# Two differential attentions in a transformer kernel: probabilities combined two steps ahead, head norms one step later, Silu in pairs, and y rows handed to the output projection as they come

## The chip, the cores and the metric

The kernel runs on one core of a Trainium2 chip. The time is device time in microseconds (us), a median over runs of the same program. The engines have their own instruction streams and wait for one another by semaphores: TensorE (PE in the profile, its weight loads PEld), VectorE (DVE), ScalarE (ACT), GpSimd (POOL), and SyncE (SP), which issues most DMAs.

## The reference

Two transformer blocks in float32 over 256 tokens of width 2048. The first block has two layers. Each layer normalises its input, multiplies by `w_in`, and mixes three branches, each with a Silu gate: attention, pooling and convolution. Layer 0 does it for 256 tokens of x and 256 of a context; layer 1 for x alone (the keys and values still cover both). What the change touches:

```python
def _diff_attention(q, k, v, lam):          # 8 heads, per head two scores of depth 64
    s = jnp.einsum('bqhcd,bkhcd->bhcqk', qq, k).astype(jnp.float32) * scale
    p = jax.nn.softmax(s, axis=-1)
    a = p[:, :, 0] - lam * p[:, :, 1]
    return jnp.einsum('bhqk,bkhe->bqhe', a.astype(v.dtype), v)
...
    y_att = (_rmsnorm(o, subln_g) * (1.0 - lam_init)).reshape(B, L, ATT_WIDTH)
    ...
    y = jnp.concatenate([y_att * jax.nn.silu(g_att),
                         y_pool * jax.nn.silu(g_pool),
                         y_conv * jax.nn.silu(g_conv)], axis=-1)
    return y @ w_out
```

## The kernel before

All large products go by units of weights: one unit is 128 output features by 2048 inputs (1 MB). SyncE loads a unit into `RAW`, ScalarE rounds it in two halves into `WH` (`high`), GpSimd subtracts to get `WL` (line 538), and TensorE makes three matmuls for each of 16 blocks: high by high, high weight by low activation, low weight by high activation (lines 574 to 576). Buffers are two deep, and the semaphores `high_ready`, `split_ready` and `halves_done` tie the three engines together. A unit has 48 matmuls: 512 columns wide in layer 0, 256 wide in layer 1.

Each layer's attention (the functions `attention(l)`, one in each engine's stream) is a hand-written software pipeline over steps `g`. Layer 0 has J = 4 query tiles per head, so 32 steps; layer 1 has J = 2, so 16 steps. `h = g // J` is the head and `s = g % J` the tile in it; in this text the steps of a head are its first, second, third and fourth. A step of TensorE is: transpose the combined probabilities of step g (line 793), scores of step g+2 (line 761), at some steps one of rotate (lines 734, 735, for the rotary embedding of a later head), `out_back` (line 769, transposes a finished head's output back) and `turn_v` (line 742, transposes the next head's values), then `gate_part`, a piece of the sixteen gate units (half a unit in layer 0, a whole one in layer 1), and last the product with the values (line 825). ScalarE copies the transposed probabilities, takes the exponentials of step g+2, does the norm of the last head's output (`head`: squares, Ln, Exp), the Silu of the gate tiles and the `high` of the weights. VectorE finds the maxima of the scores (1754), combines the two softmaxes (`RECIPROCAL` 1789, 1791, 1792, semaphore `at0_comb` or `at1_comb`), applies the rotary embedding, finishes the head norm (1763 to 1766 and a multiply, semaphore `_on`) and multiplies by the gates (1775, and `gate_mul`).

In what order VectorE does this is the point of contact. Step g of VectorE begins with the combination of step g itself; then come the maxima of g+2 and the other work. In the first step of each head that other work ends with `head(h-1)`, which waits for ScalarE's `_rr`:

```python
                if s == 0 and h:
                    head(h - 1)
                if s == 1 and h:
                    gated(h - 1)
```

After the last step, ScalarE and VectorE split the mixed rows y into `HH` and `HL` in four pieces of four tiles, and TensorE starts the output projection (`residual_tiles`), 16 tiles of `w_out`. Between these tiles it makes the modulation vectors of later stages (`mod_unit`, line 552, 1 MB of weights each), one before each tile in layer 0 (from a single buffer, `BUF_OUT0`), two before each in layer 1 (four buffers). SyncE issues the first of these loads after `at{l}_y` has reached 8, that is after the last head is gated, and each further one when TensorE has read a buffer. ScalarE issues the reload of x (`xin`, two pieces of 2 MB) at the end of layer 0's attention.

## Time and profile before

| | us |
|---|---|
| median of 3 runs | 3447.99 (3447.86 to 3456.14) |
| the profiled execution, its own time | 3441.95 |
| its span | 3440.2 |
| TensorE busy | 3184.4 (93%) |
| GpSimd busy | 1890.8 (55%) |
| ScalarE busy | 1488.4 (43%) |
| VectorE busy | 1263.8 (37%) |

Busy time is the sum of an engine's instructions; a stretch in which TensorE is busy at half its clock counts as busy too. The first attention (layer 0) lies at about 576 to 885 us of the span, the second (layer 1) at about 1508 to 1722 us, and each is followed by its output projection.

### The profile page before, as it was taken

To read this page: it belongs to the slowest core of one execution; us is meant where nothing else is said; L and a number is where in the kernel's file an instruction comes from. 1 tells how busy PE (TensorE), PEld (TensorE's weight loads), DVE (VectorE), ACT (ScalarE), POOL (GpSimd) and SP (SyncE) were. 2 spreads that over 40 slices of the span, in tenths; PEclk is the share of its full clock that TensorE was granted. 3 is DMA by queue.
4 is the path that set the end of the run, shared out by engine and by line. 5 is a ranking of instruction groups with operands and counts; after the bars stand their busy time and mean duration, and the time that the engine had idled before them with its cause. 6 is when DMAs were issued, how large, how long until landed. Compare 5 with 4: busy or idle time off the path is not lost.

```text
span 3440.2 us, 64483 instructions
## 1 busy us (share of the span) xinstructions
PE 3184.4 (93%) x25962; PEld 2845.4 (83%) x25962; DVE 1263.8 (37%) x2045; ACT 1488.4 (43%) x2186; POOL 1890.8 (55%) x756
## 2 busy tenths in 40 slices
PE   6899999998799996997799899999989999999999
PEld 4788886776677895876688788889989999999999
DVE  2148303444201418035412876667251443333000
ACT  3222223556322431256634566556534555554333
POOL 1244543222233557443344555566776888887887
PEclk9999999999899998998899999999999999999999
DMA  9786222111443781222196576544444455554555
GB/s 393 305 331 262 98 98 75 60 62 50 171 153 141 308 327 54 94 109 75 60 357 254 189 249 239 199 147 147 171 159 159 171 183 183 182 184 171 183 195 183
DMA packets 85970, 613.35 MB, mean 178 GB/s; under 512 B 9536, under 2 KB 10816, under 8 KB 12736
## 3 DMA queue, kind: packets, MB, share of 16 engines
q1 hardware_dynamic: 84672, 606.02, 47.7%
q10 hardware_dynamic: 1152, 5.24, 0.4%
q8 instruction: 109, 1.79, 0.2%
q14 instruction: 37, 0.30, 0.0%
HBM read 609.13 MB, written 2.10 MB: 178 GB/s over the span
## 4 chain that ended last, share of the span: by engine, by line
issue 59%; POOL 39%; POOLq 1%; PE 0%; DVE 0%; DVEq 0%
POOL w_low L538 39%; POOLq L533 0%; POOLq L537 0%; POOLq L538 0%; PE bank L574 0%; PE bank L576 0%; PE bank L575 0%; DVE region L2235 0%; DVEq L2235 0%; POOLq L2246 0%
## 5 line engine op out<-in xcount | busy, mean ns | idle before, releaser
L538 POOL TENSOR_TENSOR w_low<-raw,w_high 128x1024 fp32r<-128x1024 f32 x752 | 1890.6, 2527 | 1543.0 <-ACT w_high L1084 1540.1
L574 PE MATMUL bank<-h_high,w_high 128*128 128x256 f32 (+1 forms) x4480 | 1440.0, 321 | 47.5 <-POOL w_low L538 47.5
L575 PE MATMUL bank<-h_low,w_high 128*128 128x256 f32 (+1 forms) x4480 | 1415.3, 316 | 0.0
L576 PE MATMUL bank<-h_high,w_low 128*128 128x256 f32 (+1 forms) x4480 | 1414.5, 316 | 0.0
L1084 ACT ACTIVATE w_high<-raw 128x1024 fp32r<-128x1024 f32 x752 | 786.8, 1054 | 1175.2 <-PE bank L576 722.9
L574 PEld LDWEIGHTS bank<-h_high,w_high 128*128 128x128 f32 x4480 | 862.2, 192 | 126.5 <-issue 40.2
L575 PEld LDWEIGHTS bank<-h_low,w_high 128*128 128x128 f32 x4480 | 862.2, 192 | 51.8 <-issue 0.7
L576 PEld LDWEIGHTS bank<-h_high,w_low 128*128 128x128 f32 x4480 | 860.6, 192 | 53.2
L1084 ACT ACTIVATE region<-bank 128x512 f32<-128x512 f32 (+3 forms) x353 | 164.2, 472 | 421.8 <-PE bank L576 303.0
L552 PE MATMUL bank<-region,vec_sb 128*32 128x128 f32 x6016 | 195.2, 281 | 38.2 <-DMA region<-in_w_mods 38.1
L552 PEld LDWEIGHTS bank<-region,vec_sb 128*32 128x32 f32 x6016 | 162.9, 112 | 71.6 <-issue 38.8
L574 PE MATMUL bank<-ffn_high,w_high 128*128 128x256 f32 x704 | 201.3, 286 | 10.3 <-DVE ffn_low L1606 5.9
L575 PE MATMUL bank<-ffn_low,w_high 128*128 128x256 f32 x704 | 199.8, 284 | 0.0
L576 PE MATMUL bank<-ffn_high,w_low 128*128 128x256 f32 x704 | 199.8, 284 | 0.0
L1084 ACT ACT_TABLE_LOAD x128 | 164.2, 1283 | 3.3 <-PEq L2246 1.0
L574 PEld LDWEIGHTS bank<-ffn_high,w_high 128*128 128x128 f32 x704 | 135.8, 193 | 12.5 <-POOL w_low L538 6.4
L1690 DVE SCALAR_TENSOR_TENSOR region<-region,vec_sb 128x482 f32<-128x482 f32 (+29 forms) x240 | 141.7, 670 | 0.0
L575 PEld LDWEIGHTS bank<-ffn_low,w_high 128*128 128x128 f32 x704 | 135.8, 193 | 0.0
L576 PEld LDWEIGHTS bank<-ffn_high,w_low 128*128 128x128 f32 x704 | 135.7, 193 | 0.0
L2218 DVE SCALAR_TENSOR_TENSOR ffn_space<-bank,vec_sb,ffn_space 128x255 f32<-128x255 f32 x88 | 42.5, 483 | 245.0 <-ACT ffn_space L1084 245.0
L1754 DVE TENSOR_REDUCE soft_sb<-bank 128x1 f32<-128x512 f32 (+1 forms) x96 | 53.3, 597 | 187.7 <-PE bank L761 187.7
L1609 DVE TENSOR_TENSOR region<-region 128x256 f32<-128x256 f32 (+16 forms) x116 | 104.1, 931 | 3.9
(227 smaller groups left out, 3170.2 us busy)
## 6 DMA issues: line engine op xcount, KB each, us to landing
region<-in_w_mods SPq DMA_DIRECT2D x188, 1024.0 KB, 7.9
raw<-in_w_in SPq DMA_DIRECT2D x172, 1024.0 KB, 4.9
raw<-in_w_up SPq DMA_DIRECT2D x88, 1024.0 KB, 4.8
raw<-in_w_out SPq DMA_DIRECT2D x48, 1024.0 KB, 5.0
raw<-in_w_down SPq DMA_DIRECT2D x48, 1024.0 KB, 4.8
raw<-in_w_abr SPq DMA_DIRECT2D x8, 1024.0 KB, 4.9
raw<-in_w_sbr SPq DMA_DIRECT2D x8, 1024.0 KB, 4.9
region<-in_xin SPq DMA_DIRECT2D x1, 4096.0 KB, 14.8
```

Source lines behind the costliest of these rows:

```text
L538: nc.gpsimd.tensor_tensor(WL[s][:, part], RAW[s][:, part], WH[s][:, part], ALU.subtract) \
L552: last = nc.tensor.matmul(bank[32 * j:32 * j + 32, P * at:P * (at + 1)], COLS[:, 3 * k:3 * k + 32], buffer[:, P * k:P * (k + 1)], start=k ...
L574: nc.tensor.matmul(bank[:, 0:n], WH[slot][:, w], h, start=first and j == 0, stop=False)
L575: nc.tensor.matmul(bank[:, 0:n], WH[slot][:, w], l, start=False, stop=False)
L576: end = nc.tensor.matmul(bank[:, 0:n], WL[slot][:, w], h, start=False, stop=last and j == len(blocks) - 1)
L1084: return nc.scalar.activation(out, in_, func, **kw)
L1609: return V.tensor_tensor(o_, a, b, ALU.add)
L1690: own.mark(V.scalar_tensor_tensor(acc, st(uc[:, c, :])[:, :, a + off:b + off], VE[:, wdw + 31 * c + tap:wdw + 31 * c + tap + 1], acc, ALU. ...
L1754: last = V.reduce_max(MX[:, 2 * b + c:2 * b + c + 1], BANK[2 * b + c][:, 0:nk], AX)
L2218: seq(V.scalar_tensor_tensor(acc[:, 1:T], L[r][:, 0:T - 1], vec_at("conv_w", 3 * n + 1), acc[:, 1:T], ALU.mult, ALU.add))
```

## The change

It has five parts.

1. **Combination two steps ahead.** VectorE's combination becomes a function `combined(g)`; before the loop it is done for steps 0 and 1, and each step g ends with `combined(g + 2)`, behind that step's other work.
2. **Head norms a step later.** VectorE's `head(h-1)` goes from the first to the second step of head h. In layer 1 ScalarE's Ln and Exp for it (`head_roots`) come after `gate_part`, TensorE's `out_back` goes to the next head's first step (in another PSUM bank, `turned_back`), and `gated` with it. In layer 0 `out_back` goes behind `gate_part` of the same step, and `gated` one step later.
3. **Silu in pairs.** The even gate tile is copied out of PSUM without an activation function; with the odd one, two Silu are done in a row.
4. **y rows as they come.** In layer 1 ScalarE and VectorE split each finished y tile inside the attention (`head_high`, `tile_high`, `head_low`, `tile_low`); in layer 0 four pieces are split at its end, the first of them before the last head's norm.
5. **The first two tiles of the output projection** are made together, block by block (`pair_block`), each block as soon as its rows are split, and `out_back(7)` stands between the blocks. `residual_tiles(..., paired=True)` then skips these two tiles, but still calls `before` (the modulation units) for them. SyncE's and GpSimd's streams are unchanged.

The core of the diff:

```diff
+        def pair_block(u, t0_, hi, lo, t0, n, k):
+            for s in range(2):
...
-                        pe.wait_ge(bank_free[s], 1 + t0_ // 4 + i)
-                        whole(u0 + s, i, 4, L[s], s % 2, hi, lo, t0, n, ys if end == 1 and s == 0 else None)
+                        if not (paired and end == 1 and s < 2):
+                            pe.wait_ge(bank_free[s], 1 + t0_ // 4 + i)
+                            whole(u0 + s, i, 4, L[s], s % 2, hi, lo, t0, n)
...
+            pe.wait_ge(sem(nm + "_exp"), steps)
+            for kk in range(KT):
+                if l == 0:
+                    if kk == 4:
+                        pe.wait_ge(sem("at0_y"), 7)
+                        out_back(7)
+                    if kk % 4 == 0:
+                        pe.wait_ge(sem("ys0_lo" if kk < 8 else "yh0_lo"), kk % 8 // 4 + 1)
+                else:
+                    if kk == 8:
+                        out_back(7)
+                    pe.wait_ge(sem("ys1_lo" if kk < 8 else "yh1_lo"), kk - 7 if kk >= 8 else 2 * kk + 1 if kk < 4 else 2 * kk - 6)
+                pair_block(U_OUT[l], T_OUT[l], HH, HL, 0, w, kk)
...
             def gate(t):
-                if t % 2:
-                    dst = q[:, 2 * (t // 4) + t % 4 // 2, :]
-                else:
-                    dst = TEMP[:, 0:w]
-                    if t:
-                        act.wait_ge(sem(nm + "_gm"), t // 2)
-                run(dst, BANK[4][:, 0:w], ACT.Silu).then_inc(sem(nm + "_gate"), 1)
+                if t % 2 == 0:
+                    if t:
+                        act.wait_ge(sem("at_gm"), 8 * l + t // 2)
+                    run(TEMP[:, 0:w], BANK[4][:, 0:w], ACT.Copy).then_inc(sem(nm + "_gate"), 1)
+                else:
+                    run(q[:, t // 2, :], BANK[4][:, 0:w], ACT.Silu).then_inc(sem(nm + "_gate"), 1)
+                    act.wait_ge(sem(nm + "_gate"), t)
+                    run(TEMP[:, 0:w], TEMP[:, 0:w], ACT.Silu).then_inc(sem("at_silu"), 1)
...
+            for g in range(2):
+                combined(g)
             for g in range(steps):
...
+                if J == 2 and s == 0 and h >= 2:
+                    gated(h - 2)
-                if s == 0 and h:
+                if s == 1 and h:
                     head(h - 1)
-                if s == 1 and h:
+                if J == 4 and s == 2 and h:
                     gated(h - 1)
...
+                if g + 2 < steps:
+                    combined(g + 2)
```

VectorE in the second attention, one head's first step, as it is before (region2 holds q, k and v, region3 the probabilities and y; the multiply into region3 from region2 is `gate_mul`):

```order
L1609 TENSOR_TENSOR region2<-region2 128x256
L1763 TENSOR_SCALAR ss_sb<-ss_sb 128x2 [waits at1_rr,at1_qk]
L1603 TENSOR_TENSOR rr_sb<-rr_sb 128x2 [waits dve_own]
...
L1603 TENSOR_TENSOR region2<-region2,rr_sb 128x256 [waits dve_own]
L1603 TENSOR_TENSOR region3<-region3,region2 128x256 [waits at1_gate]
L1789 RECIPROCAL soft_sb<-soft_sb 128x2 [waits at1_exp]
L1791 TENSOR_SCALAR region3<-region3,soft_sb,lam_sb 128x512 [waits dve_own]
L1792 SCALAR_TENSOR_TENSOR region3<-region3,soft_sb 128x512 [waits dve_own]
```

and the same engine now, from that first step's end to the second step's end (1820 is the head norm's first line, 1845 to 1848 the combination, 1663 the new splits):

```order
L1832 SCALAR_TENSOR_TENSOR region2<-bank,sg_sb,region2 128x256 [waits at1_gate,at_ot,at1_qk]
L1845 RECIPROCAL soft_sb<-soft_sb 128x2 [waits at1_exp]
...
L1811 TENSOR_REDUCE soft_sb<-bank 128x1 [waits at1_sc,at1_comb]
...
L1820 TENSOR_SCALAR ss_sb<-ss_sb 128x2 [waits at_rr]
...
L1660 TENSOR_TENSOR region2<-region2,rr_sb 128x256 [waits dve_own]
L1660 TENSOR_TENSOR region3<-region3,region2 128x256 [waits at_silu]
L1663 TENSOR_TENSOR h_low<-region2,h_high 128x256 [waits yh1_hi]
L1663 TENSOR_TENSOR h_low<-region3,h_high 128x256 [waits ys1_hi]
L1845 RECIPROCAL soft_sb<-soft_sb 128x2 [waits at1_exp]
L1847 TENSOR_SCALAR region3<-region3,soft_sb,lam_sb 128x512 [waits dve_own]
```

The combination that stood behind the wait for `at1_rr` was that of the very next step; what stands behind it now is the one for two steps on.

TensorE at the end of the first attention before (825 the last products with the values, 769 `out_back(7)`, 552 the first modulation unit, 574 the first tile of the output projection):

```order
L825 MATMUL bank<-region 128x128 [waits at0_at]
L825 MATMUL bank<-region 128x128 x3
L769 MATMUL bank<-const_sb,region 128x128 [waits at0_on,at0_y]
L769 MATMUL bank<-const_sb,region 128x128 x3
L667 UNCONDITIONAL_BRANCH [waits at0_exp]
L552 MATMUL bank<-region,vec_sb 32x128 [waits mod_in0,mod_out]
L552 MATMUL bank<-region,vec_sb 32x128 x15
L574 MATMUL bank<-h_high,w_high 128x512 [waits split_ready,ys0_lo,bank_free0]
```

and now (831, 777, 557 and 579 are the same four lines; 600 to 602 are `pair_block`):

```order
L831 MATMUL bank<-region 128x128 [waits at0_at]
...
L600 MATMUL bank<-h_high,w_high 128x512 [waits bank_free0,split_ready,ys0_lo,at0_exp]
...
L777 MATMUL bank<-const_sb,region 128x128 [waits at_on,at0_y]
...
L600 MATMUL bank<-h_high,w_high 128x512 [waits yh0_lo]
...
L557 MATMUL bank<-region,vec_sb 32x128 [waits mod_in0,mod_out]
L557 MATMUL bank<-region,vec_sb 32x128 x15
L557 MATMUL bank<-region,vec_sb 32x128 [waits mod_in0]
L557 MATMUL bank<-region,vec_sb 32x128 x15
L557 MATMUL bank<-region,vec_sb 32x128 [waits mod_in0]
L557 MATMUL bank<-region,vec_sb 32x128 x15
L579 MATMUL bank<-h_high,w_high 128x512 [waits split_ready,bank_free2]
```

The two tiles moved ahead of the first modulation unit, and the first three modulation units now follow one another with no tile between them.

## Rows read from the trace of the kernel before

**Rows 1.** The page: engine shares, first row.
```profile
PE 3184.4 (93%) x25962; PEld 2845.4 (83%) x25962; DVE 1263.8 (37%) x2045; ACT 1488.4 (43%) x2186; POOL 1890.8 (55%) x756
```

**Rows 2.** TensorE's waits, 575 to 886 and 1508 to 1724: total, times, longest.
```profile
PE bank L793 <- DVE region L1792: 30.1, 8, 4.4
...
PE bank L793 <- DVE region L1792: 49.1, 8, 7.4
```

**Rows 3.** Windows: length, then each engine's busy, PEclk, DMA share, GB/s.
```profile
627.72:874.07 246.35, 220.05 (x1024) 169.05 (x1023) 103.59 (x237) 142.16 (x278) 61.66 (x26) 0.92 0.15 52
874.07:923.45 49.38, 31.33 (x218) 24.99 (x216) 12.75 (x17) 18.01 (x24) 9.53 (x4) 0.79 0.53 213
...
1546.39:1705.16 158.77, 118.31 (x810) 101.16 (x809) 76.63 (x141) 106.80 (x177) 57.90 (x25) 0.86 0.21 73
1705.16:1749.04 43.88, 26.46 (x322) 23.76 (x320) 14.24 (x22) 16.50 (x24) 13.69 (x6) 0.73 0.59 234
```

**Rows 4.** Timeline of TensorE, first attention: start, duration, line, operation, [idle before].
```profile
596.36 0.38 PE L793 MATMUL bank<-const_sb,region 128*128 128x128 f32 x2
...
603.75 0.60 PE L793 MATMUL bank<-const_sb,region 128*128 128x128 f32 x4
...
611.79 0.60 PE L793 MATMUL bank<-const_sb,region 128*128 128x128 f32 x4
...
619.45 0.38 PE L793 MATMUL bank<-const_sb,region 128*128 128x128 f32 x2
...
627.28 0.60 PE L825 MATMUL bank<-region 128*128 128x128 f32 x4
631.52 0.69 PE L793 MATMUL bank<-const_sb,region 128*128 128x128 f32 x2 [3.64 <-DVE region L1792]
...
640.10 0.39 PE L575 MATMUL bank<-h_low,w_high 128*128 128x512 f32 x1
640.32 0.39 PE L576 MATMUL bank<-h_high,w_low 128*128 128x512 f32 x1
```

**Rows 5.** Timeline of TensorE, second attention, heads 0 and 1.
```profile
1528.42 0.60 PE L793 MATMUL bank<-const_sb,region 128*128 128x128 f32 x4
...
1537.19 0.60 PE L793 MATMUL bank<-const_sb,region 128*128 128x128 f32 x4
...
1538.78 0.70 PE L734 MATMUL bank<-region,const_sb 128*128 128x256 f32 x2
...
1545.50 1.05 PE L825 MATMUL bank<-region 128*128 128x128 f32 x8
1553.17 1.12 PE L793 MATMUL bank<-const_sb,region 128*128 128x128 f32 x4 [6.61 <-DVE region L1792]
```

**Rows 6.** VectorE: timeline rows of both attentions, and line 1791 in 1508 to 1724.
```profile
628.74 0.17 DVE L1763 TENSOR_SCALAR ss_sb<-ss_sb 128x4 f32<-128x4 f32 x1 [4.17 <-ACT rr_sb L1084]
...
1684.46 2.37 DVE L1791 TENSOR_SCALAR region<-region,soft_sb,lam_sb 128x512 f32<-128x512 f32 x1
...
L1791 DVE TENSOR_SCALAR region<-region,soft_sb,lam_sb x16: 545/595/2370, 1515.1 to 1708.2; 128x512 f32<-128x512 f32 x16
```

**Rows 7.** Timeline of ScalarE, second attention: a table load and the Silu behind it.
```profile
1681.37 1.28 ACT L1084 ACT_TABLE_LOAD   x1
1682.67 0.38 ACT L1084 ACTIVATE region<-bank 128x256 f32<-128x256 f32 x1
```

**Rows 8.** First attention's end: timelines, and two DMA issues (886 and 911 us).
```profile
882.21 5.49 ACT L1084 ACTIVATE h_high<-region 128x2048 fp32r<-128x2048 f32 x3
...
885.96 8.89 DVE L1606 TENSOR_TENSOR h_low<-region,h_high 128x2048 fp32r<-128x2048 f32 x4
...
895.85 1.93 PE L552 MATMUL bank<-region,vec_sb 128*32 128x128 f32 x32 [10.60 <-DMA region<-in_w_mods]
...
region<-in_w_mods SPq DMA_DIRECT2D x1, 1024.0 KB, 9.4
...
region<-in_w_mods SPq DMA_DIRECT2D x1, 1024.0 KB, 4.7
```

More of the change, by code:

```diff
@@ L578, in product, with whole @@
             end.then_inc(halves_done, 1)
-        def whole(u, i, per, bank, slot, hi, lo, t0, n, ys=None):
+        def whole(u, i, per, bank, slot, hi, lo, t0, n):
             for half in range(2):
-                if ys:
-                    pe.wait_ge(ys, 2 + 2 * half)
                 pe.wait_ge(split_ready, 2 * u + half + 1 + 2 * per * i)
                 product(bank, slot, range(8 * half, 8 * half + 8), 8 * half, hi, lo, t0, n, half == 0, half == 1)
+        def pair_block(u, t0_, hi, lo, t0, n, k):
+            for s in range(2):
+                if k == 0:
+                    pe.wait_ge(bank_free[s], 1 + t0_ // 4)
+                if k % 8 == 0:
+                    pe.wait_ge(split_ready, 2 * (u + s) + k // 8 + 1)
+                h, l = (r[:, k, t0:t0 + n] for r in (hi, lo))
+                w = slice(P * k, P * (k + 1))
+                nc.tensor.matmul(L[s][:, 0:n], WH[s][:, w], h, start=k == 0, stop=False)
+                nc.tensor.matmul(L[s][:, 0:n], WH[s][:, w], l, start=False, stop=False)
+                end = nc.tensor.matmul(L[s][:, 0:n], WL[s][:, w], h, start=False, stop=k == KT - 1)
+                if k % 8 == 7:
+                    end.then_inc(halves_done, 1)
         def first_pair(u, t0_, hi, lo, t0, n, ready, k0=0, k1=KT):
@@ L591, in first_pair @@
                 pe.wait_ge(sem("n_hl"), ready + k + 1)
-                for s in range(2):
-                    if k == 0:
-                        pe.wait_ge(bank_free[s], 1 + t0_ // 4)
-                    if k % 8 == 0:
-                        pe.wait_ge(split_ready, 2 * (u + s) + k // 8 + 1)
-                    h, l = (r[:, k, t0:t0 + n] for r in (hi, lo))
-                    w = slice(P * k, P * (k + 1))
-                    nc.tensor.matmul(L[s][:, 0:n], WH[s][:, w], h, start=k == 0, stop=False)
-                    nc.tensor.matmul(L[s][:, 0:n], WH[s][:, w], l, start=False, stop=False)
-                    end = nc.tensor.matmul(L[s][:, 0:n], WL[s][:, w], h, start=False, stop=k == KT - 1)
-                    if k % 8 == 7:
-                        end.then_inc(halves_done, 1)
+                pair_block(u, t0_, hi, lo, t0, n, k)
         def two_tiles(u, t0_, hi, lo, t0, n):
@@ L795, in attention @@
                 if g + 2 < steps:
+                    if J == 2 and s == 1 and h >= 2:
+                        pe.wait_ge(sem(nm + "_y"), h - 1)
                     scores(g + 2)
@@ L1171, in residual_highs @@
                     for s in range(4):
+                        if paired and end == 1 and s == 0:
+                            pair_rest(u0)
                         if parts:
                             parts(i, s)
-                        ahead(u0 + s, s % 2, i, 4)
+                        if not (paired and end == 1 and s < 2):
+                            ahead(u0 + s, s % 2, i, 4)
                         if s or first:
@@ L1798, in attention @@
                     rope(l, h + lead)
-                if s == 0 and h:
+                if J == 2 and s == 0 and h >= 2:
+                    gated(h - 2)
+                if s == 1 and h:
                     head(h - 1)
-                if s == 1 and h:
+                if J == 4 and s == 2 and h:
                     gated(h - 1)
-                if J == 4 and g % 4 == 1:
-                    gate_mul((g - 1) // 2)
-                if J == 2 and g % 2 == 0:
-                    gate_mul(g)
-            head(7)
-            gated(7)
+                if s == J - 1:
+                    gate_mul(h)
+                if J == 2 and g == steps - 1:
+                    gated(6)
+                if J == 2 and s == 1:
+                    if h >= 2:
+                        head_low(h - 2)
+                    if h:
+                        tile_low(h - 1)
+                if g + 2 < steps:
+                    combined(g + 2)
+            if l == 0:
+                rows_low(0)
+                head(7)
+                rows_low(1)
+                rows_low(2)
+                gated(7)
+                rows_low(3)
+            else:
+                head(7)
+                head_low(6)
+                tile_low(7)
+                gated(7)
+                head_low(7)
         dve.wait_ge(sem("vec_in"), 16)
@@ L1900, in _ @@
                     dve.wait_ge(sem(name), 32 if first == 0 else 16)
-                with dve.Fori(first, end) as i:
+                if first == 0:
+                    for s in range(4):
+                        residual(0, s, x0, s < 2)
+                with dve.Fori(max(first, 1), end) as i:
                     for s in range(4):
```

179 lines of the change are left out of this document (106 added, 73 removed).

## The prediction

> **What bounds the kernel now.** I read the page first. TensorE is busy for 93% of the span [rows 1] and no other engine comes near, so only what makes TensorE idle, or what makes its clock fall, can be won. The table of waits by engine says where TensorE idles within the two stretches that the change touches: it waits for line 1792, VectorE's combination, 8 times and 30.1 us in the first attention and 8 times and 49.1 us in the second [rows 2]. The windows give the rest of the loss. From 627.72 to 874.07 (second step of head 1 to the last gate product) TensorE is busy for 220.05 of 246.35 us, at a mean granted clock of 0.92. From 1546.39 to 1705.16, the same piece of the second attention, it is busy for 118.31 of 158.77 us at a clock of 0.86 [rows 3]. So there are 26.3 and 40.5 us without a matmul, and part of the busy time is at 1.2 GHz.
>
> The timelines show one wait and its cause. TensorE is ready for the transposes of a head's second step at 627.9 and gets them at 631.52, after 3.64 us [rows 4]; in the second attention the same wait takes 6.61 us [rows 5]. VectorE at that time stands in front of line 1763, the head norm, until ScalarE has made `rr_sb` [rows 6]. It works in order, and the combination that TensorE wants stands behind this wait. One head later it is the same: the wait comes once per head, not once per step.
>
> **The change, part by part.** *Combination two steps ahead, norm a step later.* No instruction is saved; the order alone changes. The wait for `rr` no longer stands before the combination of the next step, but before one that TensorE wants about two steps on. I price this by what steps take when nothing stalls.
>
> First attention: from 596.36 (second step of head 0) to 627.72 (end of the first step of head 1) there is no stall: four steps in 31.36 us [rows 4]. Head 0 has no `out_back` there; four transposes of that kind take 0.60 [rows 4], so a head needs 31.96. The window holds head 1 without its first step (31.96 less 8.27, which is 619.45 to 627.72), five whole heads, and head 7 to its third gate product: 31.96 less its fourth step (611.79 to 619.45, 7.66), less about 2.9 for the rotation, the last scores, `turn_v` and the values that it doesn't have. That is 23.7 + 159.8 + 21.4 = 204.9, against 246.35: 41.4 us less. A new small wait comes in: in a head's first step ScalarE makes the norm before it copies the gate tile out of the one gate bank, and TensorE wants that bank early in the second step. By the old times that copy is about 0.25 us late (before, the wait for the combination hid it): seven times, 1.8 us. First attention: **-39.6**.
>
> Second attention: a first step with rotation takes 9.2 (1537.19 to 1546.39), a second one 8.77 with `turn_v` (1528.42 to 1537.19) [rows 5]; with two transposes for `out_back`, 0.3, a head is 18.3. The window is six heads long. Less the rotations of heads 6 and 7 (the two matmuls that begin one take 0.70 [rows 5], the whole of it about 0.8), and about 2.4 of scores and values that head 7 lacks: 109.8 - 4.0 = 105.8, against 158.77: **-53.0**. Of both sums, 26 and 40 us are waits, the rest is clock. After the 6.61 us the transposes take 1.12, four of them at full clock 0.60 [rows 5]. The first stall of each attention (nothing to do before the first softmax) stays.
>
> *Can the other engines follow a head of 18.3 us?* In the window of six heads ScalarE is busy for 106.80, VectorE for 76.63, GpSimd for 57.90 [rows 3], so 17.8, 12.8 and 9.7 per head. ScalarE would be nearly full. Silu in pairs takes away what I count in its instruction order: three table loads per head in the second attention and two in the first, of 1.28 each [rows 7]. The new roundings of y tiles add two instructions like the 0.38 of [rows 7]. That leaves 17.8 - 3.84 + 0.76 = 14.7, and VectorE 12.8 + 0.8 = 13.6 with its two new subtractions. Both lie beside TensorE's 18.3, and there are two steps between a combination and its use. A load begins 1.30 before the Silu behind it [rows 7]; nothing but the load lies between. The Trainium skill ("ScalarE: Activation LUTs", What ACT_TABLE_LOAD costs) adds a drain of about 1.38 us to each table switch; by it the three loads left would cost 4.1 us more, ScalarE 18.8 per head, and the second attention would gain some 3 us less. The trace shows no such drain.
>
> *y rows and the two tiles made together.* First attention's end: before, the third tile of the projection starts at 923.45, 49.4 us after the last gate product [rows 3]; TensorE idles 10.60 of them for the first modulation load alone [rows 8]. Now, counted from 874.07: about 3 for two Silu, a rounding and a copy on ScalarE, then one piece rounded (5.49 / 3 = 1.8) and subtracted (8.89 / 4 = 2.2) [rows 8], so `pair_block` starts at +7. Its 96 matmuls at 0.225 (two starts in [rows 4]) are 21.6; the stall before costs it 2.3 of clock (41.4 us over seven heads is 5.9 each, of which 3.64 is wait), `out_back` 0.6: +32. The first modulation load is issued once head 7 is gated, at +17, and takes 9.4 [rows 8], so it is hidden. But units 2 and 3 use the same single buffer: each load starts when the unit before has been read and nothing stands between. That is twice 4.7 (the row for such a load on a quiet queue, [rows 8]) and three units of 1 to 1.9 [rows 8]: the third tile starts at +46 to +47, then runs its first matmuls at 1.2 GHz, 2.3 lost. Sum +49: **0**, from -4 (the clock stays up) to +9 (both loads take 9.4). What is late next is the modulation load; what was won by the pair is given back there.
>
> Second attention's end: 43.9 us from the last gate product to the third tile [rows 3]. Head 7 is gated at about the same distance from it as before, since the same chain of squares, Ln and Exp leads there. Six loads of 1 MB are issued at once and the third tile needs two more; at 2.4 us each they set its start, so I take **0**, from -4 to +4.
>
> **The sum.** 3441.95 - 39.6 - 53.0 = 3349.4 for the profiled execution's own time. I add 3 for waits that I can't see, since VectorE, ScalarE and GpSimd now meet at other moments: 3352. The median of the runs stands 6.0 above the profiled execution, so the forecast is **3358**. Its own range is 3345 to 3372.
>
> **The rivals.**
> *A. VectorE becomes the bound of the second attention.* Line 1791 takes 0.545 at best, but 2.37 when it meets GpSimd's subtraction, one such case is at 1684.46 [rows 6]. GpSimd is busy for 9.7 of 26.5 us per head now and will be for 9.7 of 18.3. With ten instructions per head that can meet it at up to 1.8 each, VectorE's 13.6 become at worst 31. If half of this comes true, a head takes 23 instead of 18.3: 6 x 4.7 = 28 us less gain, 3386. For it: the 2.37. Against it: 13.6 holds the present share of such waits already, and they end with one GpSimd instruction. The Trainium skill ("SBUF — State Buffer", Who interferes with whom) has the same as a rule: an exclusive lock on a shared port, which a VectorE instruction with two SBUF inputs or in a two-port mode contends for; the change adds two such per head and packs them closer. The trace agrees, with 0.545 against 2.37. Chance 0.12.
> *B. The modulation loads cost more than I take.* At 9.4 each, with the reload of x (4 MB) still in the queue, and half clock for the tile after: +15 in both ends together, 3373. Chance 0.08.
> *C. The waits go but the clock stays down.* Then only the waits are won: 72 us (79.2 of [rows 2] less the two first stalls, about 7), 3448 - 72 + 3 = 3379. Against it: between stalls the 512-column matmuls start every 0.22 us [rows 4], which is 2.4 GHz. Chance 0.04.
> *D. Slower.* At the end of each step VectorE waits for the exponentials of step g+2, and ScalarE makes them behind the work of step g. If ScalarE came a whole step late, each step would be a round trip TensorE, VectorE, ScalarE, VectorE with a stall like today's 3.64 plus 2.3 of clock. Today 14 steps of 48 stall for it; the change breaks even if another 16 did (93 / 5.9), and with all 48 it would be 34 x 5.9 - 93 = 108 slower, 3556. Against it: ScalarE is idle for a fifth of its time even in the fuller attention. Chance 0.02.
> *E. No effect,* for instance if another wait of the same length stood right behind the old one: 3448. Only ScalarE's gate copy does, with 0.25. Chance 0.02.
>
> **How the numbers follow.** My forecast has 0.72. Faster by over 0.3% (10 us, about what a measurement of this kernel can tell) are the forecast and A to C, 0.96; D is slower, 0.02; E the same, 0.02. The range goes from 3338 (both ends at their best, no extra waits, and execution to execution some 3 us) to 3392, which takes in A, B and C.
>
> **What would show it.** Right: no wait for the combination in the profile after except each attention's first; the granted clock in both attentions at 0.98 or more; heads of about 32.2 and 18.3 us; 37 table loads fewer; three modulation units in a row with two gaps of about 5 us. Wrong: VectorE without idle time in the second attention and line 1847 at over 1.4 us in the mean (A), long gaps before the modulation units (B), or TensorE waiting for `_at` copies or scores in each step (D).

## The result, and the profile after

The changed kernel takes 3356.21 us (median of 4 runs, 3353.54 to 3358.88); the kernel before took 3447.93 (4 runs, 3447.31 to 3456.14). The ratio is 0.9729, 95% interval 0.9712 to 0.9746: 93 us faster by the ratio. The forecast was 3358. The profiled execution took 3353.54, its span is 3351.8.

The page of the changed kernel, first row (against [rows 1]) and the clock in 40 slices:

```profile
PE 3164.1 (94%) x25962; PEld 2836.3 (85%) x25962; DVE 1278.4 (38%) x2057; ACT 1444.4 (43%) x2177; POOL 1894.6 (57%) x756
...
PEclk9999999999899997999898999999999999999999
```

TensorE has the same 25962 matmuls and is busy for 20.3 us less, so a part of the gain is clock: the same matmuls ran faster. The rest is idle time that is gone. The windows of the same four pieces of the program as in [rows 3] say where (second step of head 1 to the last gate product, and from there to the third tile of the output projection; first attention, then second):

```profile
628.40:833.53 205.13, 204.19 (x1024) 159.35 (x1023) 112.49 (x230) 126.44 (x270) 61.91 (x26) 1.00 0.18 62
833.53:880.69 47.16, 31.39 (x218) 25.20 (x216) 13.79 (x18) 19.10 (x26) 11.71 (x5) 0.82 0.56 223
1506.86:1612.41 105.55, 105.07 (x807) 94.05 (x805) 82.56 (x145) 86.27 (x173) 58.01 (x24) 1.00 0.32 111
1612.41:1656.00 43.59, 27.38 (x323) 24.61 (x321) 6.87 (x25) 15.98 (x29) 13.11 (x6) 0.77 0.58 239
```

The first attention went from 246.35 to 205.13 us and the second from 158.77 to 105.55. TensorE is now idle for 0.9 and 0.5 us in them, where it was idle for 26.3 and 40.5, and the granted clock is 1.00 in both. The two ends hardly moved: 49.38 to 47.16, and 43.88 to 43.59.

TensorE's waits over the whole span, against [rows 2] (line 801 is the old 793, 1848 the old 1792, 557 the old 552, 579 the old 574):

```profile
PE bank L557 <- DMA region<-in_w_mods: 38.8, 18, 6.4
...
PE bank L801 <- DVE region L1848: 7.1, 2, 3.8
```

The wait for the combination is left twice: the first of each attention, which nothing covers. The other fourteen, 72 us, are gone.

### The profile page after: what moved, and what is told of

It reads as the page before. It is cut to its first block, busy times and chain, and to the rows that moved or that the text cites. A ratio compares the mean times of both kernels' runs of the same rounds, so it can differ in the third digit from the quotient of the medians.

```text
span 3351.8 us, 64404 instructions
## 1 busy us (share of the span) xinstructions
PE 3164.1 (94%) x25962; PEld 2836.3 (85%) x25962; DVE 1278.4 (38%) x2057; ACT 1444.4 (43%) x2177; POOL 1894.6 (57%) x756
## 4 chain that ended last, share of the span: by engine, by line
issue 58%; POOL 40%; POOLq 1%; PE 0%; DVE 0%; DVEq 0%
POOL w_low L543 40%; POOLq L538 0%; POOLq L542 0%; POOLq L543 0%; PE bank L579 0%; PE bank L581 0%; PE bank L580 0%; DVE region L2332 0%; DVEq L2332 0%; POOLq L2343 0%
## 5 line engine op out<-in xcount | busy, mean ns | idle before, releaser
L579 PE MATMUL bank<-h_high,w_high 128*128 128x256 f32 (+1 forms) x4416 | 1415.3, 320 | 48.5 <-POOL w_low L543 47.1
L580 PE MATMUL bank<-h_low,w_high 128*128 128x256 f32 (+1 forms) x4416 | 1393.4, 316 | 0.0
L581 PE MATMUL bank<-h_high,w_low 128*128 128x256 f32 (+1 forms) x4416 | 1393.3, 316 | 0.0
L579 PEld LDWEIGHTS bank<-h_high,w_high 128*128 128x128 f32 x4416 | 848.0, 192 | 136.8 <-issue 44.2
L581 PEld LDWEIGHTS bank<-h_high,w_low 128*128 128x128 f32 x4416 | 847.4, 192 | 51.0
L580 PEld LDWEIGHTS bank<-h_low,w_high 128*128 128x128 f32 x4416 | 848.1, 192 | 49.8 <-issue 0.7
L1795 DVE TENSOR_TENSOR mod_sb<-bank,vec_sb 128x12 f32<-128x12 f32 (+1 forms) x48 | 8.1, 169 | 267.1 <-PE bank L565 267.0
L2332 DVE SCALAR_TENSOR_TENSOR region<-bank,mod_sb,region 128x256 f32 x16 | 7.7, 484 | 256.4 <-PE bank L581 256.4
```

The costliest lines, as they stand in the source:

```text
L579: nc.tensor.matmul(bank[:, 0:n], WH[slot][:, w], h, start=first and j == 0, stop=False)
L580: nc.tensor.matmul(bank[:, 0:n], WH[slot][:, w], l, start=False, stop=False)
L581: end = nc.tensor.matmul(bank[:, 0:n], WL[slot][:, w], h, start=False, stop=last and j == len(blocks) - 1)
L1795: V.tensor_tensor(MODF[:, ds(3 * n, 12)].rearrange("p (n c) -> p n c", c=3), bank[:, 0:16].rearrange("p (n c) -> p n c", c=4)[:, :, 0:3], ...
L2332: V.scalar_tensor_tensor(tile(RES, n), L[s][:, 0:T], MODF[:, ds(3 * n + 3 * 176 + 2, 1)], tile(RES, n), ALU.mult, ALU.add).then_inc(bank_f ...
```

## The experiments

All times of kernels are medians; ratios are to the kernel before, measured on the same chip (there at 3445.84, 3448.6 and 3447.14 us in the three groups). A difference of two kernels in us is their difference of ratios times 3448. Each ratio has an interval of about 0.0016 to either side, so such a difference is known to about 8 us; for the small ones I give the length of the stretch in the traces beside it.

### The combination's place: `e1_no_lookahead`

```diff
-            for g in range(2):
-                combined(g)
             for g in range(steps):
+                combined(g)
...
-                if g + 2 < steps:
-                    combined(g + 2)
```

> The changed kernel with one thing undone: VectorE combines step g at the start of step g again; the norm stays in the second step. Theory 1 (what counts is that no combination stands behind the wait for the norm's inverse root when TensorE wants it; either of the two reorderings does that): the first attention keeps its 205 us. In the second, the combination of a first step now stands behind the two subtractions of the second step, which wait for ScalarE; those end about 8 us after TensorE began the step, the combination takes 1.5 to 3.5 more, and TensorE wants it at 8.3: a wait of 1.4 to 3.3 us per head and perhaps 2.3 of clock, 10 to 30 us in all, so 3366 to 3386. Theory 2 (looking two steps ahead is what removes the stalls): the stalls of the kernel before come back in both, 3430 to 3450. Theory 3 (only the norm's place counts): 3356.

The wait ahead of the maxima is adapted (`g + 1` instead of `g + 2`). Measured 3369.87, ratio 0.9778 (0.9762 to 0.9794): 17 us over the changed kernel. In the first attention only the first stall is there (3.8 us). In the second (1470 to 1640):

```profile
PE bank L801 <- DVE region L1848: 15.1, 7, 3.2
```

One of the seven is the first stall, 3.2. So the norm's new place alone, without the lookahead, takes away every later stall of the first attention and leaves six of 1.7 to 2.0 us in the second. VectorE ahead of one of them:

```profile
1538.76 2.74 DVE L1848 SCALAR_TENSOR_TENSOR region<-region,soft_sb 128x512 f32<-128x512 f32 x1
```

It ends at 1541.50, and TensorE, ready at 1539.53, starts at 1541.56. The same instruction takes 0.75 us when it runs alone; here it meets GpSimd's subtraction, which starts at 1538.60. All six stalls have a combination of 2.7 us ahead of them, and in the other ten steps line 1848 takes 0.75. Without the collision it would have ended at 1539.51, in time (an estimate from these rows). So in the second attention the lookahead is worth what it hides of that collision. From the second step of head 0 to the last step (starts of the transposes) `e1` takes 138.39 us and the changed kernel 124.41: 14.0 of the 17 us lie there, 0.4 in the same stretch of the first attention. Of the theories the first holds, with waits of the length that it gave.

### The norm's place: `e2_norm_early`, `e9_dve_norm_early`, `e10_act_roots_early`

`e2` keeps the lookahead and puts the norm back on both engines; `e9` does the first half of this edit alone, `e10` the second.

```diff
 # VectorE, both attentions
-                if s == 1 and h:
+                if s == 0 and h:
                     head(h - 1)
 # ScalarE, second attention
+                    if s == 0 and h:
+                        head_roots(h - 1)
                     gate_part(g + 1)
-                    if s == 0 and h:
-                        head_roots(h - 1)
```

> The changed kernel with the norm in the first step of the next head again, on VectorE in both attentions and on ScalarE (Ln and Exp before the gate part) in the second; the combination stays two steps ahead. Theory 1: VectorE waits for the inverse root, but what stands behind it is wanted two steps later, so no stall of TensorE for a combination; ScalarE frees the gate bank later in the second attention (about 0.8 us per head). 3356 to 3366. Theory 3 (only the norm's place counts): the stalls come back, 3430 or more.

Measured 3376.88, ratio 0.9803 (0.9786 to 0.9821): 26 us over the changed kernel, where my theory had at most 10. The combination's stalls were gone as expected. TensorE waited elsewhere in the second attention (1505 to 1680):

```profile
PE bank L579 <- ACT region L1102: 14.7, 5, 3.0
...
PE bank L831 <- ACT region L1102: 2.7, 2, 1.9
PE bank L750 <- DVE region L1666: 2.2, 2, 1.1
```

The largest is the one gate bank, which ScalarE's copy frees, and in this kernel Ln and Exp with their table loads stand ahead of that copy. I took that for the cause, and the two halves were run to see whether it is.

> The changed kernel with VectorE's head norm (waiting for rr) back in the first step of a head in both attentions; the two-step lookahead stays, and ScalarE's Ln and Exp stay behind the gate part in the second attention. It is one half of the edit that put both norms back and measured 3377, some 20 over the changed kernel, and it asks which half cost the 20. Theory 1, ScalarE's half did it (Ln and Exp ahead of the gate part keep TensorE from its one gate bank, 2.9 a head): here no wait for the gate bank in the second attention, heads of 18.2 to 19, and 0 to 6 us over the changed kernel, 3354 to 3362. Rival, VectorE's half did it: VectorE now waits for rr in the first step, the maxima of the step after and with them ScalarE's exponentials come later, and the gate copy with them: since Ln and Exp are later still here than with both put back, then at least 15 over, 3370 or more, with TensorE waits behind maxima, scores or the gate bank.

> The changed kernel with ScalarE's Ln and Exp of the head norm put ahead of the gate part in the second attention alone; VectorE's order stays as changed. Theory 1, this half cost the 20 us: waits for the gate bank of 2 to 3 us in most heads of the second attention, heads of 21 to 24 instead of 18.2, and 12 to 20 us over the changed kernel, 3367 to 3376. Rival: it costs only what two small ScalarE instructions and their table loads take ahead of a copy that has time to spare, under 4 us in all, 3354 to 3360.

`e9` measured 3383.63, ratio 0.9809 (0.9793 to 0.9824): 28 us over the changed kernel. `e10` measured 3364.41, ratio 0.975 (0.9735 to 0.9765): 7 over. VectorE's half costs as much as both, so theory 1 fell for the most part and its rival holds. Of ScalarE's half the times alone allow anything from 0 to 15 us; in the traces its second attention (same stretch as above) takes 134.87 us, 10.5 over the changed kernel, which is less than I expected of it and more than its rival. VectorE in `e9`, one head from one combination to the next head's:

```profile
1546.01 2.79 DVE L1848 SCALAR_TENSOR_TENSOR region<-region,soft_sb 128x512 f32<-128x512 f32 x1
...
1553.18 0.48 DVE L1832 SCALAR_TENSOR_TENSOR region<-bank,sg_sb,region 128x256 f32<-128x256 f32 x1
1560.41 0.17 DVE L1820 TENSOR_SCALAR ss_sb<-ss_sb 128x2 f32<-128x2 f32 x1 [6.75 <-ACT rr_sb L1102]
...
1568.56 2.79 DVE L1848 SCALAR_TENSOR_TENSOR region<-region,soft_sb 128x512 f32<-128x512 f32 x1
```

The head takes 22.55 us instead of 18.2. VectorE stands 6.75 of them in front of the norm. TensorE waits at most 0.3 us for a combination, so that is not what is late: it is the maxima of the next step (line 1811) that stand behind, and ScalarE's exponentials wait for those. The waits of VectorE and then of ScalarE in `e9` (1508 to 1640), and under them, apart, the same two of the changed kernel (1508 to 1620, a shorter stretch):

```profile
DVE ss_sb L1820 <- ACT rr_sb L1102: 44.0, 6, 8.9
...
ACT region L1102 <- DVE soft_sb L1813: 42.0, 11, 4.0
```

```profile
DVE ss_sb L1820 <- ACT rr_sb L1102: 11.1, 7, 7.7
...
ACT region L1102 <- DVE soft_sb L1813: 16.8, 5, 3.6
```

I read this as a ring: VectorE waits for ScalarE's root, ScalarE in its next step for VectorE's maxima, and a lateness goes round once per head. TensorE shows it only as small waits spread over several lines (1505 to 1680 in `e9`), the largest 2.4 us:

```profile
PE bank L742 <- ACT region L1102: 5.5, 4, 1.8
...
PE bank L579 <- ACT region L1102: 4.9, 5, 1.9
PE bank L777 <- ACT region L1102: 3.6, 2, 2.4
PE bank L750 <- DVE region L1666: 3.3, 3, 1.1
PE bank L801 <- DVE region L1848: 1.0, 4, 0.3
```

These come to 18.3 us. From the second step of head 0 to the last step `e9` takes 151.24 us (1493.90 to 1645.14) and the changed kernel 124.41, 26.8 more, which is nearly the whole loss. TensorE is idle for 18.4 us of it instead of 0.5. The other 9 us are busy time (132.80 against 123.93): the same matmuls at a granted clock of 0.95 instead of 1.00. `e2` takes 149.63 us for the same stretch, 25.2 more; VectorE waits less for the root (25.7 us in 8), since Ln and Exp are earlier, and TensorE more for the gate bank. That is why the halves do not add up. `e10` has three waits for the gate bank, 7.4 us in all, and its heads take alternately about 22 and 18.3 us. In the first attention neither `e2` nor `e9` loses anything (237.5 us for the same stretch, as in the changed kernel's 237.4): there the norm's early place costs TensorE no wait once the combination is two steps ahead.

### The order undone on both: `e7_order_undone`

The edits of `e1` and `e2` together; Silu in pairs, the y rows and the pair of tiles stay.

> Both reorderings undone together, all else of the change kept (Silu in pairs, y rows as they come, the pair of tiles). Theory 1: 7 stalls of 3.6 us in the first attention and 6 or 7 of 3 to 6 us in the second are back, each with 2.3 us of clock behind it: 75 to 95 us over the changed kernel, 3430 to 3450. Rival (a good part of the gain comes from fewer table loads or from the split rows): 3356 to 3400.

Measured 3459.3, ratio 1.0046 (1.0029 to 1.0063): 16 us slower than the kernel before, some 10 above what I expected. So the order is worth 109 us in this setting, more than the whole gain, and the other parts win nothing without it. TensorE's waits in the first attention (575 to 890) and in the second (1500 to 1730):

```profile
PE bank L801 <- DVE region L1848: 42.7, 8, 6.3
...
PE bank L801 <- DVE region L1848: 46.0, 14, 6.5
```

Against [rows 2] the first attention waits 12.6 us more for the same eight stalls: the seven later ones are 5.5 to 6.3 us instead of 3.6 to 4.4. VectorE ahead of one of them, and GpSimd in the same stretch:

```profile
671.70 0.16 DVE L1845 RECIPROCAL soft_sb<-soft_sb 128x2 f32<-128x2 f32 x1
671.89 2.24 DVE L1847 TENSOR_SCALAR region<-region,soft_sb,lam_sb 128x256 f32<-128x256 f32 x1
...
671.50 2.48 POOL L543 TENSOR_TENSOR w_low<-raw,w_high 128x1024 fp32r<-128x1024 f32 x1 [7.89 <-ACT w_high L1102]
```

The awaited combination now runs into GpSimd's subtraction and ends with it (674.13 and 673.98). Line 1847 takes 2.2 us ahead of each of the seven later stalls; before, the same instruction (line 1791) took 0.41 there. That is the 16 us: from the first transposes to the last, the first attention takes 303.34 us where the kernel before took 288.55, 14.8 more. The second takes 193.5 where it took 194.8. Its stalls are fourteen instead of eight, but six of them are only 0.4 to 0.8 us long, and the transposes behind these take 0.66 us, not the 1.12 of a long stall.

### The norm alone, in the kernel before: `e5_norm_moved_alone`

```diff
-                if s == 0 and h:
+                if s == 1 and h:
                     head(h - 1)
-                if s == 1 and h:
                     gated(h - 1)
```

> The kernel before with one edit: VectorE's head norm goes from a head's first step to its second, ahead of the multiply by the gate; TensorE's and ScalarE's order stay. Theory: the stall moves. TensorE's transposes get their probabilities in time, but its transposes of the finished head stand in front of the gate product and now wait for the norm, which comes behind the maxima: about 3.3 us in each head of both attentions. First attention as before, second some 3.3 us less per head: 3420 to 3445. Rival (the place of the norm on VectorE alone is enough): 3350 to 3370.

Measured 3441.69, ratio 0.9981 (0.9971 to 0.9991): 7 us, where the whole change gives 93. TensorE in 575 to 900, then in 1500 to 1730 (769 is `out_back`, 793 the transposes of the combination):

```profile
PE bank L769 <- DVE region L1603: 42.6, 8, 6.7
PE bank L793 <- DVE region L1792: 3.8, 1, 3.8
...
PE bank L769 <- DVE region L1603: 38.8, 8, 5.7
...
PE bank L793 <- DVE region L1792: 3.3, 1, 3.3
```

The stall for the combination is gone and stands at `out_back` instead, since TensorE asks for the normed head at the old place. (One of the eight in each attention, 6.7 and 5.7 us, is `out_back(7)`, which waited as long before.) From the first transposes to the last, the first attention takes 7.7 us more than before, the second 15.8 less. Here rival E of the prediction came true. In the changed kernel it did not, because `out_back` went later as well; `e1`, with both later, has no such stall.

### Silu one by one: `e3_silu_each`

```diff
-                    run(TEMP[:, 0:w], BANK[4][:, 0:w], ACT.Copy).then_inc(sem(nm + "_gate"), 1)
+                    run(TEMP[:, 0:w], BANK[4][:, 0:w], ACT.Silu).then_inc(sem(nm + "_gate"), 1)
...
-                    run(TEMP[:, 0:w], TEMP[:, 0:w], ACT.Silu).then_inc(sem("at_silu"), 1)
+                    act.sem_inc(sem("at_silu"), 1)
```

> The changed kernel with a Silu for each gate tile by itself, straight from PSUM, as before; all else kept. That puts one table load of 1.28 us more per even tile ahead of the copy that frees the gate bank, and one to go back to Exp. First attention: the bank is free about 1.6 us after TensorE wants it, 7 times, 11 us. Second: ScalarE goes from 14.4 to about 17.6 us of 18.2 per head; 0 to 15 us. Theory (pairs are needed once the stalls are gone): 3366 to 3382. Rival (ScalarE has room for the loads): 3356. If each switch also cost a drain of 1.4 us, over 3390.

Measured 3364.54, ratio 0.976 (0.9742 to 0.9779): 11 us over the changed kernel, where from 8 us on a difference is clear of noise; the traces have 11.6 (the first attention from its second step to its last, 248.99 against 237.41). That is far under the 3390 of a drain at each switch. TensorE in 575 to 860:

```profile
PE bank L579 <- ACT region L1102: 10.9, 7, 2.3
```

So the pairs are worth about 11 us, all of it in the first attention, where a table load ahead of the gate copy keeps TensorE from the gate bank in each of seven heads. In the second attention such waits come to 0.6 us. I had given the pairs a place in the sum only as room on ScalarE there.

### The projection's first tiles as before: `e4_old_end`

`pair_block` and `paired=True` are taken out of all engines' streams; the first two tiles are made one after the other in `residual_tiles` again.

> The changed kernel without its pair of tiles: after the attention TensorE transposes the last head, waits for the first modulation unit and makes the first tiles of the projection one after the other, as before; the y rows are still split as they come. Theory (what the pair wins is given back by the modulation loads that now follow one another): third tile of the first projection 49 us after the last gate product instead of 47.2, of the second 43 to 44 as now: 3356 to 3362. Rival (the pair saves the 10 us of idle time before the first modulation unit): 3366 to 3376.

Measured 3358.4, ratio 0.9738 (0.9719 to 0.9757): 3 us over the changed kernel, no difference that this measurement can tell. At the first attention's end in `e4` TensorE waits 15.7 us once for the first modulation load and 7.1 for `out_back(7)`; the changed kernel waits 11.4 for the loads of the second and third unit:

```profile
864.36 1.08 PE L557 MATMUL bank<-region,vec_sb 128*32 128x128 f32 x32
871.83 1.94 PE L557 MATMUL bank<-region,vec_sb 128*32 128x128 f32 x32 [6.38 <-DMA region<-in_w_mods]
878.82 1.93 PE L557 MATMUL bank<-region,vec_sb 128*32 128x128 f32 x32 [5.06 <-DMA region<-in_w_mods]
```

The pair hides one load and lays two bare. No run takes out the y rows split as they come (part 4), so what they are worth alone is not shown.

### These loads earlier: `e6_mods_earlier`

In layer 0 the second and third modulation unit get buffers of their own, in space that is free once the last y rows are split, and the second half of x is loaded after they are read. In layer 1 two of the first four loads are issued once `out_back` of head 3 is done.

```diff
+                    mod_load(BUF_OUT0[0], 0, M_OUT0)
+                    unit(0, 2)
+                    sp.wait_ge(sem("yh0_lo"), 2)
+                    for s in (1, 2):
+                        sp.dma_start(R2[:, UNIT * (s - 1):UNIT * s], mods[M_OUT0 + s]).then_inc(sem(f"mod_x{s}"), 16)
...
+                if l == 1:
+                    sp.wait_ge(sem("at_ot"), 8 + 4)
+                    mod_load(BUF_OUT1[0], 0, M_OUT1)
+                    mod_load(BUF_OUT1[2], 2, M_OUT1 + 2)
```

> The changed kernel with the modulation loads of both projections made earlier: in the first, units 1 and 2 go to space of their own once all y rows are split, so that three loads lie beside the pair of tiles, and the second half of x is loaded after they are read; in the second, two of the four buffers are filled during the attention. Theory (those loads in a row are what holds the third tile back): the gaps of 6.4 and 5.1 us go and with them 2 to 3 of clock, first end 47 to 33, second end 43.6 to 33 or 36: 20 to 27 us faster, 3329 to 3336. Rival (something else is late there, the weights' split or the reload of x): less than 8 us.

Measured 3338.56 (3332.79 to 3338.99), ratio 0.9675 (0.9659 to 0.9692); the changed kernel, run again on the same chip as `e8_after_again`, took 3354.39, ratio 0.9728 (0.9712 to 0.9745). So it is 16 us faster by the medians (18 by the ratios), the best version, ahead of both kernels. That is clear of the rival's 8 and short of the theory's 20 to 27: counted from the last gate product, the third tile starts at 35.7 in the first end and 38.6 in the second, where I had 33 and 33 or 36. TensorE at the first end in `e6` (590 and 695 are the modulation units, 612 the third tile):

```profile
868.32 1.08 PE L590 MATMUL bank<-region,vec_sb 128*32 128x128 f32 x32
869.22 1.06 PE L695 MATMUL bank<-region,vec_sb 128*32 128x128 f32 x32
872.19 1.08 PE L695 MATMUL bank<-region,vec_sb 128*32 128x128 f32 x32 [1.92 <-DMA region<-in_w_mods]
873.20 0.50 PE L612 MATMUL bank<-h_high,w_high 128*128 128x512 f32 x1
```

Between the start of the first modulation unit and the third tile lie 4.9 us here and 16.3 in the changed kernel (864.36 to 880.69). Of the difference, 9.5 us are wait (6.38 and 5.06 there, 1.92 here), and 1.7 are two units at 1.94 and 1.93 us that take 1.06 and 1.08 here: behind the waits of 6.38 and 5.06 the granted clock is 0.50, behind the 1.92 it is 1.00. At the second end TensorE still waits 3.3 us for a load, and the third tile starts 5 us earlier than in the changed kernel.

> The changed kernel again, on the same chip as the three above: 3353 to 3359.

## Why the prediction was right

**The first attention** was put at -39.6 and came to -41.2. Heads take 31.89 us (660.29 less 628.40, the starts of two heads' second steps) against 31.96. Of the seven small waits for the gate bank, 1.8 in the sum, one came, 0.88. That is 0.9 of the 1.6 between forecast and result, and the shorter heads are 0.4.

**The second attention** was put at -53.0 and came to -53.2. The head, 18.3 in the sum, is 18.2 (1533.39 to 1551.58, the starts of two heads' second steps). Two things in the reading of the stalls were too simple, though the sum doesn't hang on them. VectorE's wait for `rr` is only the start of a stall. In the first attention 0.8 of the 3.64 us are that wait (TensorE is ready at 627.9, `rr` comes at 628.74) and the rest is VectorE's norm and combination. In the second, `rr` is there at 1545.96, before TensorE is ready at 1546.56; the 6.61 us are VectorE's own work, and two of its instructions meet a subtraction of GpSimd (1546.88 to 1549.23, 1549.52 to 1552.04):

```profile
1545.96 0.17 DVE L1763 TENSOR_SCALAR ss_sb<-ss_sb 128x2 f32<-128x2 f32 x1 [3.44 <-ACT rr_sb L1084]
...
1546.96 2.55 DVE L1603 TENSOR_TENSOR region<-region,rr_sb 128x256 f32<-128x256 f32 x1
...
1549.95 2.37 DVE L1791 TENSOR_SCALAR region<-region,soft_sb,lam_sb 128x512 f32<-128x512 f32 x1
```

Alone they take 0.43 and 0.55 us, so 3.9 of the 6.61 are these collisions. What the new order took off TensorE's path was this work as much as the wait for `rr`. The second point is the 2.3 us of clock behind a stall: it holds for stalls of 3.6 us, but the stalls of 2.03 us in `e1` lengthen a head by 2.26 (20.45 against 18.19), and in the whole step behind one the granted clock is 1.00.

What carried both numbers was the method: the step without a stall was in the trace of before, in head 0, at full clock, and only had to be repeated. So the clock's share needed no term of its own.

**The room on the other engines** was well sized: per head of the second attention ScalarE 86.27 / 6 = 14.4 (14.7 forecast), VectorE 82.56 / 6 = 13.8 (13.6), GpSimd 9.7 (9.7); 37 table loads fewer (128 to 91), as counted. The table loads cost what the rows of before had them cost. ScalarE of the changed kernel:

```profile
1562.40 1.28 ACT L1102 ACT_TABLE_LOAD   x1
1563.69 0.29 ACT L1102 ACTIVATE ss_sb<-ss_sb,vec_sb 128x2 f32<-128x2 f32 x1
1564.01 1.28 ACT L1102 ACT_TABLE_LOAD   x1
1565.30 0.20 ACT L1102 ACTIVATE rr_sb<-ss_sb 128x2 f32<-128x2 f32 x1
```

From the start of a load to the start of the next instruction pass 1.29 us, and the first load starts 0.02 us after the instruction ahead of it ends (1561.33 + 1.05). The further drain of about 1.38 per switch that the Trainium skill has ("ScalarE: Activation LUTs", What ACT_TABLE_LOAD costs) isn't there, and the measurement decides.

**The ends** were put at 0 each and came to -2.2 and -0.3. In the first, `pair_block` starts at +7.0 (840.50; forecast +7), the first modulation unit follows at +30.8 with no wait (+32), the two gaps are 6.38 and 5.06 (4.7 each), and the third tile starts at +47.2 (+46 to +47, plus 2.3 of clock). What the pair won was given back at the modulation loads, as the text said; `e4` shows it from one side and `e6` from the other.

**The allowance** of 3 us for waits not seen was too small in this execution: the four pieces come to -96.9, the span to -88.4, so 8.5 us are lost elsewhere. 0.7 of it lies before the first window. 3.2 lies between the first end and the second attention; the last wait before the second attention, in the changed kernel and in the one before (its line 727 is now 735), shows most of it:

```profile
1460.18 5.41 PE L735 MATMUL bank<-region,raw 128*128 128x256 f32 x16 [2.09 <-DVE region L1789]
```

```profile
1500.80 3.72 PE L727 MATMUL bank<-region,raw 128*128 128x256 f32 x16 [1.09 <-DVE region L1732]
```

The wait is 1.0 longer and the 16 matmuls behind it take 1.7 more. The change doesn't touch them; `e1` has them at 3.72 after a wait of 1.94, `e8` at 5.41 after one of 1.88 and `e6` at 5.41 after one of 2.26, so why they fall on the one side or the other stays open. The last 4.6 lie behind the second end (1695.8 us from the third tile to the end of the span, 1691.2 before). The same kernel in `e8` took 1692.4 there, so most of it is the difference from one execution to another. The median stood 2.7 us above the profiled execution instead of the 6.0 taken. So the forecast's distance of 2 us is three errors that nearly cancel: the four pieces 4.3 us better (96.9 against 92.6), the rest 5.5 worse, the median 3.3 better. That is partly luck. The range's lower bound is also off by its own terms: 3358 less 8 for both ends, 3 for no extra waits and 3 for the execution is 3344, not 3338.

**The rivals.** A (VectorE the bound) did not happen, though its collision did. VectorE's combination in the second attention, before (1508 to 1724) and, under it, now (1470 to 1630):

```profile
L1791 DVE TENSOR_SCALAR region<-region,soft_sb,lam_sb 128x512 f32<-128x512 f32 x16 | 21.6, 1350 | 0.6
```

```profile
L1848 DVE SCALAR_TENSOR_TENSOR region<-region,soft_sb 128x512 f32<-128x512 f32 x16 | 37.0, 2315 | 0.6
...
L1847 DVE TENSOR_SCALAR region<-region,soft_sb,lam_sb 128x512 f32<-128x512 f32 x16 | 8.8, 553 | 0.6
```

The sign named for A, line 1847 over 1.4 us, did not show; it would have told little, since the same instruction had a mean of 1350 ns before (the 595 in [rows 6] is the median of the sixteen). The next line shows the collision: 2315 ns in the mean where it takes 0.75 us alone (`e9`, the same instruction at 1562.52), because it meets GpSimd's subtraction in twelve of sixteen steps. VectorE at 1551.18, and GpSimd:

```profile
1551.18 2.75 DVE L1848 SCALAR_TENSOR_TENSOR region<-region,soft_sb 128x512 f32<-128x512 f32 x1
```

```profile
1551.03 5.16 POOL L543 TENSOR_TENSOR w_low<-raw,w_high 128x1024 fp32r<-128x1024 f32 x2 [4.62 <-ACT w_high L1102]
```

GpSimd's first of the two ends at 1553.39, VectorE's instruction at 1553.93. The collisions of this line come to 1.6 x 16 = 25 us, but they are not new work: before, the collisions of line 1791 (16 x 0.8) and of the norm's multiply (a mean of 1754 ns over its eight) came to about as much, and VectorE's busy time in the window rose only from 76.63 to 82.56. What changed is where they fall. Now they cost TensorE nothing, since two steps lie between a combination and its use. It fits the rule of the exclusive lock that the prediction cited from the Trainium skill ("SBUF — State Buffer", Who interferes with whom). B (dearer loads) did not happen: 6.38 and 5.06 are far from two of 9.4. C (clock stays down) did not: 1.00. D (slower) did not: ScalarE waits for VectorE, not TensorE for ScalarE. But a ring of this kind is possible: `e9` shows one that goes round once per head instead of once per step, and costs 28 us. E holds for a part of the change (`e5`), not for the whole.

**What the prediction did not see** is how the parts hang together, since it priced them as one. Against the kernel before, the norm later without lookahead gives 76 us (`e1`), the lookahead without the later norm 66 to 68 (`e9`, `e2`), both 93; with neither, the rest costs 16, since the awaited combination of the first attention now meets GpSimd's subtraction (`e7`); which of the remaining parts moves it there, no run shows.

## What to carry to other kernels

When an engine that works in order stands in front of a wait, ask what is behind it for every engine, not only for the one that stalls: in `e9` the combination had two steps to spare, and the maxima behind the wait still cost 28 us. Moving a wait's owner alone moves the stall (`e5`); the consumer has to be moved with it. Look also at what VectorE shares with GpSimd on that path: the same collision costs 2 us a time where TensorE waits for the instruction (`e1`) and nothing where it doesn't. To price a stall's removal, take a stretch of the same work without a stall from the same trace: it holds the clock's share too.

## What the runs showed of the hardware

Which VectorE instruction meets GpSimd's subtraction depends on when it runs, and so on the order and on the parts around it: `e7` has the old order on VectorE's path, but not the old meetings. Before, line 1791 of the second attention was met in seven of sixteen steps (2.37 us each, 1350 ns in the mean), now line 1848 in twelve (2315 ns), and in `e7` line 1847 at the worst place (2.24 us ahead of an awaited combination). The busy time of VectorE rose by 14.6 us over the whole kernel ([rows 1] against the page above), which is no measure of what the collisions cost.

In two executions of the same program, the changed kernel's profile and that of `e8`, the same step of the first attention starts at 628.40 and 631.37 us, and the stretch from the third tile of the second projection to the end takes 1695.8 and 1692.4. Differences of 3 us in one profiled stretch are therefore no finding.

Behind a wait of 3.64 or 6.61 us of the kernel before TensorE went on at half clock (the transposes at 1553.17 run at a granted clock of 0.50). Behind waits of 2.03 us (`e1`, 1541.56 to 1551.47) and 1.92 us (`e6`, 872.19) it stayed at 1.00. So the clock's share of a stall is not a fixed sum per stall.
